# Delta rule, the chunk of the meta tokens: products, copies and additions of the inverse in 16 of 64 columns

## What is computed

```
L = 16 + 256 tokens, pad = 64 - 16 = 48 zero rows ahead, 5 chunks of 64
gcum  = cumsum(g);  decay = exp(where(causal, gcum_t - gcum_s, -inf))
kb    = k * beta
m     = where(strict, (kb @ k^T) * decay, 0)
sol   = solve((m + I) x = [v * beta, kb * exp(gcum)])     # unit lower triangular
u, w  = sol
v_new = u - w @ S
o     = (q * exp(gcum)) @ S + ((q @ k^T) * decay) @ v_new
S     = S * exp(g_last) + (k * exp(g_last - gcum))^T @ v_new
```

## Time and profile before

| | |
|---|---|
| median of three runs | 1663.57 us (1662.13, 1663.57, 1666.88) |
| the profiled execution | 1663.52 us |
| its span, first to last instruction | 1661.8 us |
| mean granted TensorE clock | 0.991 |
| TensorE busy | 1603.5 us, 96% of the span |
| TensorE weight loads | 1435.4 us, 86% |
| VectorE busy | 1169.3 us, 70% |
| ScalarE busy | 907.4 us, 55% |
| GpSimd busy | 74.1 us, 4% |
| HBM read, written | 227.30 MB, 1.05 MB |

### The profile page before, as it was taken

One profiled execution on the slowest core, in us unless ns is written; L12 is line 12 of the kernel. 1 busy time (PEld: TensorE's weight loads), 2 busy tenths in 40 slices (PEclk: granted clock), 3 DMA queues, 4 the chain that ended last, 5 costly groups with the idle time before them and its releaser, 6 DMA issues. The chain is left out here.

```text
span 1661.8 us, 33818 instructions
## 1 busy us (share of the span) xinstructions
PE 1603.5 (96%) x12970; PEld 1435.4 (86%) x12970; DVE 1169.3 (70%) x2011; ACT 907.4 (55%) x1622; POOL 74.1 (4%) x41
## 2 busy tenths in 40 slices
PE   7999899999999999999999999998999999999998
PEld 6888788999999999998888888887667889988877
DVE  5678566689888999986666666655765657656565
ACT  4357554454555767766566656653664645334443
POOL 0000000200000000000000000000001333200000
PEclk9999999999999999999999999999999999999999
DMA  6642255565654444446666666643122444300014
GB/s 224 190 134 86 89 165 152 168 187 160 188 183 150 142 129 139 130 139 206 197 191 192 193 195 190 192 134 98 57 75 75 152 152 152 118 25 3 3 32 147
DMA packets 63222, 230.02 MB, mean 138 GB/s; under 512 B 7024, under 2 KB 7280, under 8 KB 63104
## 3 DMA queue, kind: packets, MB, share of 16 engines
q1 hardware_dynamic: 63104, 228.37, 44.3%
HBM read 227.30 MB, written 1.05 MB: 137 GB/s over the span
## 5 line engine op out<-in xcount | busy, mean ns | idle before, releaser
L1140 DVE TENSOR_TENSOR tile_low<-weights,tile_high 128x1024 fp32r<-128x1024 f32 x252 | 308.0, 1222 | 141.3 <-ACT tile_high L1130 141.2
L1130 ACT ACTIVATE tile_high<-weights 128x1024 fp32r<-128x1024 f32 x252 | 268.0, 1064 | 134.0 <-issue 134.0
L183 ACT ACTIVATE tile_high<-weights 128x1024 fp32r<-128x1024 f32 x169 | 178.5, 1058 | 239.5 <-issue 62.9
L195 DVE TENSOR_TENSOR tile_low<-weights,tile_high 128x1024 fp32r<-128x1024 f32 x146 | 179.9, 1233 | 138.7 <-ACT tile_high L183 121.9
L1212 PE MATMUL banks<-parts,tile_high 128*128 128x256 f32 x2048 | 272.0, 286 | 0.9 <-ACT tile_high L1130 0.6
L1212 PEld LDWEIGHTS banks<-parts,tile_high 128*128 128x128 f32 x2048 | 255.3, 192 | 1.7 <-issue 1.7
L1532 PE MATMUL banks<-tile_high,parts 128*128 128x512 f32 x1024 | 253.0, 389 | 0.9 <-ACT parts L1490 0.9
L1532 PEld LDWEIGHTS banks<-tile_high,parts 128*128 128x128 f32 x1024 | 192.2, 188 | 40.9 <-issue 1.1
L237 PE MATMUL banks<-parts,tile_high 128*128 128x272 f32 (+1 forms) x1216 | 168.5, 291 | 2.3 <-ACT big L317 2.3
L237 PEld LDWEIGHTS banks<-parts,tile_high 128*128 128x128 f32 x1216 | 157.2, 190 | 11.3 <-issue 7.5
L1217 PE MATMUL banks<-parts,tile_low 128*128 128x256 f32 x1024 | 144.3, 284 | 4.1 <-DVE tile_low L1140 4.0
(11 more groups left out here) (402 smaller groups left out, 2177.7 us busy)
## 6 DMA issues: line engine op xcount, KB each, us to landing
weights<-in_peer_u SPq DMA_DIRECT2D x128, 512.0 KB, 3.6
weights<-in_peer_v SPq DMA_DIRECT2D x128, 512.0 KB, 3.5
weights<-in_dn_in SPq DMA_DIRECT2D x49, 512.0 KB, 3.5
weights<-in_in_t SPq DMA_DIRECT2D x19, 512.0 KB, 3.5
weights<-in_attn_t SPq DMA_DIRECT2D x19, 512.0 KB, 3.6
weights<-in_in_m SPq DMA_DIRECT2D x16, 512.0 KB, 3.7
weights<-in_wq SPq DMA_DIRECT2D x16, 512.0 KB, 3.7
weights<-in_dn_out SPq DMA_DIRECT2D x16, 512.0 KB, 3.5
```

The source lines that it names most:

```text
L183: k.nc.scalar.activation(k.high[:, m % 2, :], k.ring.view(n), ACT.Copy).then_inc(*k.high_made.up())
L195: unit.tensor_tensor(k.low[:, m % 2, :], k.ring.view(n), k.high[:, m % 2, :].bitcast(F32), ALU.subtract).then_inc(*k.low_made[engine].up())
L1130: k.nc.scalar.activation(k.high[:, (s + j) % 2, :], k.ring.buf[:, j % RING, :], ACT.Copy).then_inc(k.high_made.sem, 1)
L1140: k.nc.vector.tensor_tensor(k.low[:, (s + j) % 2, :], k.ring.buf[:, j % RING, :], k.high[:, (s + j) % 2, :].bitcast(F32), ALU.subtract).th ...
```

## The change

In chunk 0 the matmuls of `square` and `grow` stream the last 16 of 64 columns and write 16 columns of PSUM; the weights keep their 64 columns. `take_power` copies, and `add_inverse` adds, only these 16 columns of each head's 64. For the other chunks the same columns as before are used. The number and order of instructions and all waits stay.

```diff
             def square(c, l, b):
+                part = slice(PAD if c == 0 else 0, CH)
...
-                        ins = nc.tensor.matmul(ps[mine(o), b, at_:at_ + CH], power_of(c, o, i, 1 - a),
-                                               power_of(c, o, i, a), start=True, stop=True)
+                        ins = nc.tensor.matmul(ps[mine(o), b, at_ + part.start:at_ + CH], power_of(c, o, i, 1 - a),
+                                               power_of(c, o, i, a)[:, part], start=True, stop=True)
...
             def grow(c, l, b):
+                part = slice(PAD if c == 0 else 0, CH)
...
-                    ins = nc.tensor.matmul(ps[mine(o), 2 + b, at_:at_ + CH], power_of(c, o, i, 0),
-                                           k.R[mine(o), i, :], start=True, stop=True)
+                    ins = nc.tensor.matmul(ps[mine(o), 2 + b, at_ + part.start:at_ + CH], power_of(c, o, i, 0),
+                                           k.R[mine(o), i, part], start=True, stop=True)
...
-                R = flat(k.R[:, H * b:H * b + H, :])
-                nc.vector.tensor_tensor(R, R, ps[:, 2 + b, 0:4 * CH], ALU.add).then_inc(*rtaken.up())
+                part = slice(PAD if c == 0 else 0, CH)
+                R = k.R[:, H * b:H * b + H, part]
+                grown_by = ps[:, 2 + b, 0:4 * CH].rearrange("p (i n) -> p i n", i=H)[:, :, part]
+                nc.vector.tensor_tensor(R, R, grown_by, ALU.add).then_inc(*rtaken.up())
...
-                nc.scalar.activation(k.powers[:, c % 2, 2 * b:2 * b + 2, 0:kinds, :],
-                                     bank(b).rearrange("p (x a n) -> p x a n", x=2, a=2)[:, :, 0:kinds, :], ACT.Copy).then_inc(*ptaken.up())
+                if c:
+                    dst = k.powers[:, c % 2, 2 * b:2 * b + 2, 0:kinds, :]
+                    src = bank(b).rearrange("p (x a n) -> p x a n", x=2, a=2)[:, :, 0:kinds, :]
+                elif kinds == 2:
+                    dst = k.powers[:, 0, 2 * b:2 * b + 2].rearrange("p q a (y n) -> p (q a y) n", y=2)[:, :, PAD:CH]
+                    src = bank(b).rearrange("p (z n) -> p z n", n=CH)[:, :, PAD:CH]
+                else:
+                    dst = k.powers[:, 0, 2 * b:2 * b + 2, 0, :].rearrange("p q (y n) -> p q y n", y=2)[:, :, :, PAD:CH]
+                    src = bank(b).rearrange("p (x a y n) -> p x a y n", x=2, a=2, y=2)[:, :, 0, :, PAD:CH]
+                nc.scalar.activation(dst, src, ACT.Copy).then_inc(*ptaken.up())
```

## The result

The changed kernel is slower: 1668.66 us, the median of nine runs, against 1664.45 us of the kernel before. The ratio is 1.0025, interval 1.0015 to 1.0036; it leaves out one of the nine executions of the kernel before, which took 7135 us. The forecast was 1662.8 us, and the measured time lies 0.7 us above the stated range.

What follows compares the result with a forecast made beforehand. TensorE, busy 96% of the span, was taken to bound the kernel. Savings of 0.29 (products), 0.20 and 0.20 (additions) and 0.02 us (last growth product) sum to 0.71, giving 1662.8 us, range 1661.0 to 1668.0.

Steps and rivals of the forecast that it cites:

- The bound and the carrying over: TensorE bounds the kernel, busy 96% of the span; the delta stage's gain or loss is handed on whole.
- a queue without a hole up to 1465.90: In chunk 0, TensorE's weight loads were read as running unbroken from 1456.90 us until the query sums end.
- The holes and the additions: Two shorter VectorE additions shrink TensorE's waits before chunk 0's transposes and solve, 0.20 us each.
- The copies: ScalarE's shorter copies of chunk 0's powers lie under TensorE's queue: gain 0, between 0 and 0.1 us.
- The products: 192 narrower square and growth instructions in chunk 0 save 1.5 ns each: 0.29 us, between 0.17 and 0.56.
- it takes columns away and no time: Rival: chunk 0's loads hold 28.7 ns and additions cost nearly the same; gain 0 to 0.3 us, 1663.4, chance 0.12.
- The clock: Rival: narrow matmuls in chunk 0 halve TensorE's clock; 1664.5, 1666.2 or 1671.6 us; chance 0.24 short, 0.15 longer.
- Two row halves stream in turn: Argument against a clock fall: chunk 0's narrow matmuls alternate between two row halves; no size given.
- 1.73 us of L1951 at 16 columns: Argument against a clock fall: this narrow run at 1183.09 us stayed at granted clock 1.00 up to 1186.40.
- the L660 run that was not followed by a fall: Argument against a clock fall: a 30-column run at 90.00 us, equal to one followed by clock 0.50, had none.
- The price per microsecond: Cost of half clock on TensorE's full queue in chunk 0: 3.4 us lose 1.7 us, 6.8 us lose 3.4.

Runs made afterwards that it cites:

- e1: Changed kernel with chunk 0's matmuls streaming all 64 columns again, only copies and additions at 16; ratio to the kernel before 1.0004.
- e3: Changed kernel with chunk 0's matmuls streaming 32 columns instead of 16, copies and additions still at 16; ratio to the kernel before 1.0002.
- e8: Changed kernel with only the first level's squares of chunk 0 back at 64 columns, the rest at 16; ratio to the kernel before 1.0004.
- e7: Changed kernel with chunk 0's matmuls streaming 24 columns instead of 16; ratio to the kernel before 1.0014.
- e9: Changed kernel with only the first level's squares at 16 columns, chunk 0's other matmuls at 64, copies and additions at 16; ratio to the kernel before 1.0009.
- e2: The changed kernel measured again without any edit; ratio to the kernel before 1.0029.
- e4: Changed kernel plus two wide filler matmuls in TensorE's holes, ahead of chunk 0's transposes and first squares; ratio to the kernel before 1.0038.
- e5: Changed kernel with growth products and additions back at 64 columns, only squares and their copies at 16; ratio to the kernel before 1.0013.

## Why the prediction was wrong

**The bound and the carrying over** were right. TensorE's queue set the chunk's time, and what chunk 0 lost came out at the end whole: with 4.20 us lost there and 1.98 won ahead of it, the span grew by 2.2. (That 4.20 is also the 4.21 us between the medians is partly chance, since the falls differ from one execution to the next.) One reading was too smooth: the weight loads are not a queue without a hole up to 1465.90. At the key sums they stand 0.24 us twice, while the matmuls of 512 columns run. TensorE as a whole had no idle time there, and the sum does not change by it. Of the kernel before:

```profile
1460.85 0.19 PEld L2301 LDWEIGHTS banks<-big 128*128 128x128 f32 x1 [0.24 <-issue]
1461.28 0.86 PEld L2301 LDWEIGHTS banks<-big 128*128 128x128 f32 x7 [0.24 <-issue]
```

**The holes and the additions** were right: 0.41 us in e1, forecast 0.20 + 0.20. An addition took 0.22 us, forecast 0.21. **The copies** were worth nothing, as foretold; the row of one is 0.28 us, forecast 0.27.

**The products** were mis-sized: 0.29 us forecast, 0.08 us by e3 against e1 and 0.12 by e8 against e1 (16.46 - 16.34). The pace of 28.7 ns held with 16, 24, 32 and 64 columns. I had scaled the pair L751 and L2381 down to 0.9 ns and then moved towards L1951 without a row for it; the lower bound, 0.17 us, was still too high. What held here was the rival "it takes columns away and no time", as far as the products go. The Trainium skill, page TensorE: Matmul & The Clock Gate, section "Step-by-step: what each phase is for", says that a weight load's time goes by its column count. The constant pace agrees: the weights had 64 columns in all four cases, and only the streamed columns changed.

**The clock** is the step that failed. The sum went by a granted clock of 1.00 in chunk 0 and so put its cost at nothing; in the two profiles of the change it was 0.50 for 10.2 and 13.6 us, which cost 4.7 and 5.7 us. The mechanism stood among the rivals with the right place, the right sign and a row that shows it, but with a chance of 0.39 in all, and only 0.15 for more than one stretch. Measured lengths lie between the 6.8 us (1666.2) and the whole rest of the chunk (1671.6) that the rival had priced, and in e7 even the whole rest came.

Three reasons for the caution do not hold. "Two row halves stream in turn" was no protection. That 1.73 us of L1951 at 16 columns had no fall behind them does not carry over either: in e9 the 64 narrow instructions, 1.99 us of loads, had one right behind them, while in e8 up to 2.4 us of narrow ones in a row had none in the one profile. So the length of a narrow piece does not sort the cases. And the L660 run that was not followed by a fall I took for evidence that half of such runs are harmless. The profile of e3 shows the same first run of L660, untouched by the edit (it starts at 90.68 there), with a fall that begins a microsecond before its end:

```profile
90.30:93.70 3.40, 3.40 (x31) 3.35 (x30) 3.30 (x6) 1.73 (x3) 0.00 (x0) 1.00 0.03 10
93.70:97.10 3.40, 3.40 (x18) 3.40 (x18) 3.23 (x6) 2.14 (x4) 0.00 (x0) 0.50 0.76 194
```

In the kernel before the first of these stretches had 1.00 too, and so had the next:

```profile
93.10:96.50 3.40, 3.40 (x28) 3.36 (x28) 3.13 (x7) 1.72 (x3) 0.00 (x0) 1.00 0.79 247
```

One and the same run of matmuls is followed by a fall in one execution and not in the next, so one quiet profile clears nothing.

The price per microsecond was near: a full queue loses half, 0.5, and measured are (21.07 - 16.4) / 10.2 = 0.46, (22.10 - 16.4) / 13.6 = 0.42, (25.14 - 16.4) / 20.5 = 0.43, with 16.4 us for the same chunk at full clock (e3). What I missed is how long a fall can last, against a gain of 0.5. That narrow matmuls take longer at half clock and so hold it down is only a guess: in the changed kernel the first fall ended at 1463.6 with narrow products still to come.

That the low clock is the cause is shown by e1 against the change, which differ in streamed columns alone (e1's interval ends at 1.0018, that of e2, timed beside it, begins at 1.0019), and by the profiles, in which the same instructions take longer just where the clock is at half. The two groups of e7 agree. Ahead of the falls the engine was busy or nearly so, for 2.70 to 3.40 of 3.40 us, and what the edits changed were the streamed columns; more than that is not shown. What decides in a given execution whether and where the clock falls stays open. Why the pace stays at 28.7 ns and not at the 25.8 ns of L1951 halved stays open too.

A version that beats both cannot be named by the times. In their traces e8 and e3 are 0.5 us shorter in chunk 0 than the kernel before (16.34 and 16.38 against 16.87 us), 0.03% of the whole, and by their ratios, with intervals of some 0.1% each way, neither can be told from 1.

## What to carry to other kernels

Cutting the streamed columns of matmuls whose weights stay whole saved no time here, since the weight loads set the pace: compare the pace of two rows with equal weights before counting on it. It can cost the clock, and a queue that never idles did not protect it. Look for narrow matmuls ahead of a fall of the granted clock anywhere in the trace, and weigh some microseconds at half speed, not the one stretch seen, against the gain; and take more than one profile, since the same program has the fall in one execution and not in the next. The cut in the additions was the useful part, 0.41 us of chunk 0 by e1's trace and too little for its times to show, and it can be had alone.

## What the runs showed of the hardware

With 32 of 64 columns the profile showed no fall in chunk 0; with 24 the times of twelve executions fell into two halves 4.3 us apart; with 16 both profiles had two falls. A fall behind narrow work lasted up to 20.5 us, six times the 3.4 us of the single ones. All those of chunk 0 ended in or behind wide matmuls, the key sums or the solve, but in e7 the key sums lay in the middle of the fall and did not end it. The first fall of e4 had no idle time of TensorE ahead of it, from the start of the second filler at 1456.17 to the fall at 1460.50. The Trainium skill, page TensorE: Matmul & The Clock Gate, section "What's actually happening", has the clock follow how busy the array is; here TensorE was busy for 3.40 of 3.40 us by its records ahead of the fall in e4 and e5, so the busy time that a profile prints did not tell whether the clock would hold.
